# Moving the second norm and its transposes into the expert loop's last turn

## The reference

```python
out = jnp.zeros((n, d), h.dtype).at[tok_sorted].add(y_sorted)      # expert sums
...
x = layer_norm(DEEPNORM_ALPHA * h + ffn + ple, ln2_g[i], ln2_b[i]) # the second norm
...
u = rmsnorm(h, norm1_w[l])                                         # h = x
proj = jnp.einsum('bsd,de->bse', u, w_in[l])
```

## Time and profile before

| | |
|---|---|
| median of 3 runs | 2085.56 us |
| lowest, highest | 2081.64, 2090.03 us |
| profiled execution | 2083.52 us |
| its span | 2081.7 us |
| PE busy | 2048.2 us, 98% |
| DVE, ACT busy | 1549.3 us (74%), 1136.2 us (55%) |
| end of the last block's matmuls | 1387.5 us |
| first projection tile | 1414.9 us |

### The profile page before, as it was taken

One profiled execution on the slowest core, in us unless ns is written; L12 is line 12 of the kernel. 1 busy time (PEld: TensorE's weight loads), 2 busy tenths in 40 slices (PEclk: granted clock), 3 DMA queues, 4 the chain that ended last, 5 costly groups with the idle time before them and its releaser, 6 DMA issues.

```text
span 2081.7 us, 26318 instructions
## 1 busy us (share of the span) xinstructions
PE 2048.2 (98%) x9292; PEld 1630.0 (78%) x9292; DVE 1549.3 (74%) x1431; ACT 1136.2 (55%) x1054; POOL 242.0 (12%) x249
## 2 busy tenths in 40 slices
PE   8999999999999999999999999989999999999998
PEld 5864478888888888888888888867888878888887
DVE  6987299999999999999999999986675443333333
ACT  3132177777777777777777777754114632222222
POOL 0006211111112121211111111110000000000000
PEclk9999999999999999999999999999999999999999
DMA  5233399999999999999999999951122213222321
GB/s 226 91 142 121 137 402 396 396 384 379 383 382 379 381 380 383 378 384 378 385 375 387 376 386 375 386 196 61 66 92 86 82 41 112 101 101 83 120 81 41
DMA packets 79063, 522.31 MB, mean 251 GB/s; under 512 B 10353, under 2 KB 10881, under 8 KB 22049
## 3 DMA queue, kind: packets, MB, share of 16 engines
q1 hardware_dynamic: 66496, 483.88, 59.5%
q0 software_dynamic: 9056, 30.62, 5.7%
q10 hardware_dynamic: 3456, 7.06, 1.0%
HBM read 500.92 MB, written 18.60 MB: 250 GB/s over the span
## 4 chain that ended last, share of the span: by engine, by line
PE 94%; DVE 4%; ACT 1%; issue 1%; DMA 0%; DVEq 0%; SPq 0%; ACTq 0%
PE bank L1108 26%; PE bank L1110 26%; PE bank L1109 26%; PE bank L1100 5%; PE bank L1117 1%; PE bank L1295 1%; PE bank L1444 1%; PE bank L1247 1%; PE bank L1287 1%; PE bank L1146 1%; PE bank L1523 1%; PE bank L1504 1%; PE bank L1539 1%; PE bank L1486 0%; PE bank L1513 0%
## 5 line engine op out<-in xcount | busy, mean ns | idle before, releaser
L1848 DVE TENSOR_TENSOR ring_r<-ring,room_r 128x2048 fp32r<-128x2048 f32 x384 | 874.9, 2293 | 76.1 <-ACT room_r L765 70.4
L765 ACT ACTIVATE room_r<-ring 128x2048 fp32r<-128x2048 f32 x384 | 736.1, 1918 | 173.6 <-PE bank L1110 164.9
L1109 PE MATMUL bank<-ring_r,room_r 128*128 128x512 f32 x1744 | 678.8, 389 | 0.0
L1108 PE MATMUL bank<-room_r 128*128 128x512 f32 x1576 | 623.1, 395 | 2.3 <-DVE ring_r L1848 2.1
L1110 PE MATMUL bank<-room_r 128*128 128x512 f32 x1568 | 611.4, 390 | 0.0
L1109 PEld LDWEIGHTS bank<-ring_r,room_r 128*128 128x128 f32 x1744 | 327.8, 188 | 69.0 <-issue 3.1
L1108 PEld LDWEIGHTS bank<-room_r 128*128 128x128 f32 x1576 | 295.9, 188 | 65.2 <-DVE ring_r L1848 4.6
L1110 PEld LDWEIGHTS bank<-room_r 128*128 128x128 f32 x1568 | 294.3, 188 | 62.7
L1108 PE MATMUL bank<-room_r,ring_r 128*128 128x512 f32 x520 | 203.6, 391 | 1.8 <-DVE room_r L2193 0.9
L1110 PE MATMUL bank<-room_r,ring_r 128*128 128x512 f32 x512 | 199.3, 389 | 0.0
L1109 PE MATMUL bank<-ring_r 128*128 128x512 f32 x384 | 149.4, 389 | 0.0
(11 more groups left out here) (291 smaller groups left out, 2142.9 us busy)
## 6 DMA issues: line engine op xcount, KB each, us to landing
ring<-in_wmoe SPq DMA_DIRECT2D x384, 1024.0 KB, 12.2
ring<-in_wf SPq DMA_DIRECT2D x33, 1024.0 KB, 4.8
ring<-in_wd SPq DMA_DIRECT2D x7, 2048.0 KB, 9.2
ring<-in_wp SPq DMA_DIRECT2D x14, 1024.0 KB, 5.0
ring<-in_wo SPq DMA_DIRECT2D x2, 2048.0 KB, 9.2
ring<-in_wd SPq DMA_DIRECT2D x2, 1024.0 KB, 8.7
room<-in_xtok ACTq DMA_DIRECT2D x1, 2048.0 KB, 12.9
h_rows<-room POOLq DMA_DIRECT2D x4, 512.0 KB, 3.0
```

Of the source, the lines that this page charges most:

```text
L765: act.activation(w_hi[s_ % PAIRS], raw_w[ORDER[s_]], ACT.Copy)\
L1108: pe.matmul(out, x_hi, w_hi, start=start, stop=False, skip_group_check=True)
L1109: pe.matmul(out, x_hi, w_lo, start=False, stop=False, skip_group_check=True)
L1848: dve.tensor_tensor(w_lo[i], raw_w[i], w_hi[s_ % PAIRS].bitcast(F32), ALU.subtract)\
```

## The change

On ACT, PE and DVE the work behind the loop, up to `uT_hi`, the second projection tile and `uT_lo`, becomes a function `second_block_rows`, which is called inside `If(T < b + ROUNDS)`, at the end of the last turn that has work. On PE `p_tile(0)` and `p_tile(1)` go with it. The turns that only count thus come after that work and ahead of `half_hi(2)` on ACT, of `p_tile(2)` on PE and of `half_lo(2)` on DVE. On DVE the row selection also goes ahead of `half_lo(0)`. SP and POOL stay as they are, and no instruction is added or taken away.

```diff
@@ ACT
+            def second_block_rows():
+                deviation(0)
+                mean_square(0)
...
+                for k in range(KT):
+                    act.wait_ge(s["unT_ready"], k + 1)
+                    act.activation(uT_hi[:, k, :], bank[k][:, :], ACT.Copy, scale=pcol("norm1", k)).then_inc(s["uT_done_a"], 1)
...
                     with act.If(T < b + ROUNDS):
                         rest_act(T)
-            deviation(0)
-            mean_square(0)
...
+                        second_block_rows()
             half_hi(2)
@@ PE
+            def second_block_rows():
+
+                pe.wait_ge(s["sel_ready"], T + 1)
+                pe.wait_ge(s["x2_ready"], X2_FIRST[TT - 1])
+                for i in range(TT):
+                    pe.wait_ge(s["un_ready"], i + 1)
+                    for k in range(KT):
+                        ins = pe.transpose(bank[k][:, i * P:(i + 1) * P], un[:, i, k * P:(k + 1) * P], ident)
...
                         token_sums(T)
+                        second_block_rows()
+                        p_tile(0)
+                        p_tile(1)
...
-            for j in range(9):
+            for j in range(2, 9):
                 p_tile(j)
@@ DVE
+            def second_block_rows():
+
+                dve.wait_ge(s["late_in"], 48)
+                dve.wait_ge(s["idx_kept"], T * 2)
+                step(dve.tensor_copy(token_of[0:CAP, :], idx_row[0:CAP, :]))
+                dve.tensor_scalar(token_sel[0:CAP, :], token_row[0:CAP, :], token_of[0:CAP, :], None, ALU.is_equal)\
+                   .then_inc(s["row_sel_ready"], 1)
+                half_lo(0)
+                half_lo(1)
+                combine(0)
+                second_norm(0)
...
+                for k in range(KT):
+                    dve.wait_ge(s["uT_done_a"], k + 1)
+                    dve.scalar_tensor_tensor(uT_lo[k], bank[k][:, :], pcol("norm1", k), uT_hi[:, k, :].bitcast(F32),
+                                             ALU.mult, ALU.subtract).then_inc(s["uT_done_v"], 1)
...
                     with dve.If(T < b + ROUNDS):
                         rest_dve(T)
-            half_lo(0)
-            dve.wait_ge(s["late_in"], 48)
...
+                        second_block_rows()
             half_lo(2)
```

More of the change, by code:

```diff
@@ L855, in block_act, with deviation, mean_square, normed @@
                 first_chunk(b)
+            def deviation(i):
+                act.wait_ge(s["v1_ready"], TT + i + 1)
+                act.activation(rstd[:, i:i + 1], mva[:, i, 1:2], ACT.Sqrt, bias=eps_ln).then_inc(s["s2_ready"], 1)
+            def mean_square(i):
+                act.wait_ge(s["x2_ready"], X2_SECOND[i])
+                act.activation(un[:, i, :], h2[:, i, :], ACT.Square, accum_out=rstd[:, 4 + i:5 + i]).then_inc(s["ss_ready"], 1)
+                act.wait_ge(s["ss_ready"], 2 * i + 1)
+                act.activation(rstd[:, 4 + i:5 + i], rstd[:, 4 + i:5 + i], ACT.Sqrt, bias=eps_rms, scale=1.0 / D)\
+                   .then_inc(s["ss_ready"], 1)
+            def normed(i):
+                act.wait_ge(s["x2_ready"], X2_ROOT[i])
+                act.activation(un[:, i, :], h2[:, i, :], ACT.Copy, scale=rstd[:, 4 + i:5 + i]).then_inc(s["un_ready"], 1)
+            def second_block_rows():
+                deviation(0)
+                mean_square(0)
+                deviation(1)
+                normed(0)
+                mean_square(1)
+                deviation(2)
+                normed(1)
+                deviation(3)
+                mean_square(2)
+                mean_square(3)
+                for k in range(KT):
+                    act.wait_ge(s["unT_ready"], k + 1)
+                    act.activation(uT_hi[:, k, :], bank[k][:, :], ACT.Copy, scale=pcol("norm1", k)).then_inc(s["uT_done_a"], 1)
             def rest_act(b):
@@ L1384, in token_sums @@
                 sum_ended(TT - 1)
[L1386 to L1409, removed]
             def p_tile(j):
@@ L1430, in p_tile, with more_pe @@
                 ins.then_inc(s["p_ready"], 1)
+            def second_block_rows():
[5 more added lines that the diff above has]
+                        ins = pe.transpose(bank[k][:, i * P:(i + 1) * P], un[:, i, k * P:(k + 1) * P], ident)
+                        if i == TT - 1:
+                            ins.then_inc(s["unT_ready"], 1)
+            def more_pe(b):
+                with pe.If(b[0] < T):
+                    block_pe(b[0], False)
+                    if b[1:]:
+                        more_pe(b[1:])
+            with pe.Fori(1, BLOCKS + 1, ROUNDS) as b:
+                with pe.If(b <= T):
+                    more_pe([b + q for q in range(ROUNDS)])
+                    with pe.If(T < b + ROUNDS):
+                        sum_begun(0)
+                        rest_of_down(T, True)
+                        token_sums(T)
+                        second_block_rows()
+                        p_tile(0)
+                        p_tile(1)
             def level(n):
@@ L1928, in block_dve @@
                 first_chunk(b)
[L1930 to L1948, removed]
             def combine(i):
@@ L1987, in half_lo @@
                    .then_inc(s["flo_done"], 1)
-            half_lo(0)
-            dve.wait_ge(s["late_in"], 48)
[L1991 to L2011, removed]
+            def rest_dve(b):
+                activations(last, 1)
+                split_lo(b, 2, True)
+                turned_lo(last, 1)
+                split_lo(b, 3)
@@ new lines, in second_block_rows @@
+            def second_block_rows():
[8 more added lines that the diff above has]
+                second_norm(0)
+                combine(1)
+                first_root(0).then_inc(s["x2_ready"], 1)
+                second_norm(1)
+                combine(2)
+                first_root(1).then_inc(s["x2_ready"], 1)
+                combine(3)
+                second_norm(2)
+                second_norm(3)
+                first_rms(2)
+                first_rms(3)
+                for k in range(KT):
+                    dve.wait_ge(s["uT_done_a"], k + 1)
+                    dve.scalar_tensor_tensor(uT_lo[k], bank[k][:, :], pcol("norm1", k), uT_hi[:, k, :].bitcast(F32),
+                                             ALU.mult, ALU.subtract).then_inc(s["uT_done_v"], 1)
@@ L2014, in _, with more_dve @@
+            def more_dve(b):
+                with dve.If(b[0] < T):
+                    block_dve(b[0])
+                    if b[1:]:
+                        more_dve(b[1:])
+            with dve.Fori(1, BLOCKS + 1, ROUNDS) as b:
+                with dve.If(b <= T):
+                    more_dve([b + q for q in range(ROUNDS)])
+                    with dve.If(T < b + ROUNDS):
+                        rest_dve(T)
+                        second_block_rows()
             half_lo(2)
```

## The result

| | before | after |
|---|---|---|
| median of 13 runs each | 2085.27 us | 2089.72 us |
| lowest, highest | 2081.64, 2090.19 | 2086.53, 2100.95 |
| after / before | | 1.0027, 95% interval 1.0015 to 1.0039 |
| profiled execution, its span | 2083.52, 2081.7 | 2100.95, 2099.1 |
| another profiled execution of the changed kernel (*again*), its span | | 2090.76, 2088.9 |

The account below looks back on a forecast made before the run. PE was taken to bound the kernel (busy 98% of the span, 94% of the chain). The sum -1.6 + 4.1 + 1.0 = +3.5 us gave 2087.0 on the profiled run and 2089 as median, range 2081 to 2095.

Parts of the forecast that it names:

- Part 1: Seam behind the expert loop: early row selection, DVE exit out of its way; L1371 1.57 us earlier, gain 1.6 us.
- Rival D: Something other than the row selection held L1371, so the sums come no earlier: +5.1 us, 2091; chance 0.05.
- Part 2: DVE's 5.55 us exit behind the eight L2010 makes half_lo(2) 2.7 us late and tile 2 2.5 us late.
- Rival A: The exits cost nothing where they now stand; only the 1.6 us gain is left: 2084; chance 0.08.
- Part 3: ACT's exit of 4.15 us behind the eight L908, ahead of half_hi(2); covered by DVE's exit.
- Part 4: PE's exit between tiles 1 and 2 costs 1.6 us alone; the later wait, for L2031, counts instead.
- Part 5: Clock falls 2.5 us into PE's new 3.9 us idle time at tile 2; costs 1.0 us, bounds 0 and 2.7.
- rival B: Stall ahead of tile 2 without a fall of the clock: +2.5 us, 2088; chance 0.24.
- Part 6: Ten full turns of the loop each jump over 60 to 160 more instructions; hidden by queued work, cost 0.

Follow-up runs that it names:

- dve_in: Kernel before with DVE's part of the change alone, row selection ahead of the two splits included: 2087.35 us (before 2085.98).
- act_in: Kernel before with ACT's part of the change alone moved into the last turn: 2086.42 us (before 2085.98).
- a_all_bound: Changed kernel with the loops of ACT, PE and DVE ended at T + 1, so no empty turns: 2087.0 us (unedited changed kernel 2090.76).
- pe_in: Kernel before with PE's part alone (transposes, product tiles 0 and 1) moved into the last turn: 2086.32 us (before 2082.05).
- pe_rows_in: Kernel before with only PE's 32 transposes moved into the last turn, product tiles 0 and 1 left outside: 2087.29 us (before 2083.79).
- a_dve_bound: Changed kernel with DVE's loop alone ended at T + 1, so DVE has no empty turns: 2085.63 us (unedited changed kernel 2090.76).

## Why the prediction was right, and where it wasn't

The forecast was 2089.0, the median is 2089.72, and the chances had put 0.92 on a difference within 0.5%. By its own steps:

- *Part 1, gain 1.6.* Right. L1373 (L1371 before) starts 1.72 behind L1367, as reckoned, and 1.57 earlier than it did. The combine starts 3.64 us behind L1367's start where it was 5.36: 1.7. That the gain is 1.6 and not the 3.3 of idle DVE holds in dve_in as well. Rival D falls.
- *Part 2, DVE's walk ahead of half_lo(2).* Right in place and price: 5.4 us of branches, 4.22 idle (forecast 4.8). The half microsecond is the start: the walk began at 1420.4, while the last but one L2005 was still running, not with the last. Rival A falls.
- *Part 3, ACT's walk 3.5 us bare.* Wrong in size: 0.20. It began at 1416.4, when the second of eight L886 had just begun. I had started it with the last of them, although have it only behind waiting instructions and so show nothing of how far ACT's sequencer can run ahead. It made no difference, because it is covered by part 2. What does stand there is the table load, and I had left it behind half_hi(2) (act_in, a_all_bound: PE idle for 1.1 to 1.3 at tile 2 once DVE's walk is gone).
- *Part 4, PE's walk alone 1.6, the later one counts.* Right: 1.28 alone (pe_in), and in the full change PE's 3.40 is released by L2040 and not by issue. Tile 0 to tile 2 was to be 15.1 us (1413.3 to 1428.35) and was 14.53.
- *Part 5, a fall of the clock, 1.0.* It fell, as the earlier trace rows made likelier, but 2.80 us into the idle time instead of 2.5, just before tile 2. So nearly the whole fall of 3.41 met work: 1.4 and not 1.0. The first execution had the long fall, which cost 2.9. In rival B (no fall) the seam would be +1.8.
- *Part 6, longer body, cost 0.* This is the step that failed. It counted the branches and their cover of queued work, in a steady turn. It missed what happens once, a slow first branch (2.9 us reach the matmuls in *again*, 0.9 in pe_in), and 23 table loads, two a turn, that the program has as soon as ACT's part is in the body (act_in) and not without it (dve_in, pe_in). Why they are put there is not shown; it looks as if a table is loaded anew where paths with different functions meet. In the first turn they cost 0.6 to 1.1 us in the five executions that have them; in the later turns these 2.6 us hide, since ACT waits for PE there.

At the seam the sum was -1.6 + 4.1 + 1.0 = +3.5 and the trace gives -1.6 + 3.4 + 1.4 = +3.2. The forecast left out 2.9 + 0.9 in the loop: it had put the difference at 3.5, the two medians differ by 4.5, and the traces by 7.0 from 285 us on. That the median lies within a microsecond of the forecast is in part luck.

Of the Trainium skill: the rule of TensorE: Matmul & The Clock Gate, HAM oscillation, that bursts of matmuls with waits between them start cold again, held in *again* and dve_in, where the work behind the wait of 3.4 us ran at half clock, and in pe_rows_in behind one of 4.42 us. In pe_in, a_dve_bound and a_all_bound waits of 1.1 to 1.3 us at the same place had no such fall. The figure of the Trainium skill, Advanced Engine Details and Errata, Control Flow Timing, some 108 ns for a compare-and-branch, is not what these walks show: the branch at the `Fori` took 59 to 72 ns on DVE, 48 to 58 on ACT and mostly 214 on PE. An empty turn of two branches, a count and a move took 0.77 us on DVE, 0.58 on ACT and 0.74 on PE, most of it on DVE and ACT between the records, and the measured times decide.

## What to carry to other kernels

A loop with a fixed upper bound and a run-time end has to be left somewhere, and the empty turns cost an engine their whole time wherever its queue is short when they begin. Moving work across that point moves the price to the next wait; ending the loop at the run-time count removes it, with one line per engine (here 1.6 us at the sums in three traces, too little to show in the medians). Ahead of moving code into a loop body, ask what each turn now jumps over or loads again, and look for instructions that the diff didn't write.

## What the runs showed that I had not expected

- Moving ACT's work with other functions under an `If` in the loop's body brought 23 table loads of 1.28 us into the loop's turns, for a change that adds no instruction.
- A jump of PE over the last turn's rest takes 0.24 us; with 80 more matmuls in it, its first one took 1.9 to 3.9 us and ended 1.44 to 1.51 us after a packet of the instruction queue; with 32 more it took 0.24. The packet that looked like the extra one came 4 us too late to be the cause: times, not counts, tell.
- Sequencers run ahead by different amounts in the same stretch: PE's walk began 4.1 us before its queued matmuls ended, ACT's 4.0 us before its activations did, DVE's 1.2 us.
- Code under a condition that never holds (`T < 1`) left no branch in the trace and no other record: 26318 instructions with and without it. A padding must be seen in the instruction count before its time says anything.
